# Decode attention of a hybrid MLA decoder step: keys as the moving operand, with heads on PSUM partitions

## The reference, cut to what matters

```python
past_ckv = cache_ckv_l[page_table].reshape(db, -1, KV_LORA)
past_kr = cache_kr_l[page_table].reshape(db, -1, ROPE_DIM)
q_abs = jnp.einsum('bthd,khd->bthk', q_nope, w_uk)
s_past = jnp.einsum('bthk,bsk->bhts', q_abs, past_ckv) + jnp.einsum('bthr,bsr->bhts', q_rope, past_kr)
s_new = jnp.einsum('bthk,bsk->bhts', q_abs, ckv) + jnp.einsum('bthr,bsr->bhts', q_rope, kr)
...
sc = jnp.concatenate([s_past, s_new], axis=-1).astype(jnp.float32) * SM_SCALE
p = jax.nn.softmax(sc, axis=-1).astype(ckv.dtype)
o_lat = (jnp.einsum('bhts,bsk->bthk', p[..., :n_past], past_ckv)
         + jnp.einsum('bhts,bsk->bthk', p[..., n_past:], ckv))
o = jnp.einsum('bthk,khv->bthv', o_lat, w_uv)
```

## Time and profile before

| | us |
|---|---|
| runs before | 1612.63, 1633.86, 1609.82; median 1612.63 |
| span of the profiled execution | 1616.8 |
| TensorE matmuls, busy | 1483.7 (92% of the span) |
| VectorE, ScalarE, GpSimd, busy | 780.6, 651.9, 493.5 |
| output stage | from 1210 to the end |

### The profile page before, as it was taken

How to read it: one execution, slowest core, us unless ns; L and a number is a source line. 1 busy time by engine, 2 the same in 40 slices (tenths; PEclk the granted TensorE clock), 3 DMA queues, 4 the chain that set the end, 5 groups by cost and what they waited for, 6 DMA issues and landing times. The chain is left out here.

```text
span 1616.8 us, 24423 instructions
## 1 busy us (share of the span) xinstructions
PE 1483.7 (92%) x8584; PEld 1236.4 (76%) x8584; DVE 780.6 (48%) x1594; ACT 651.9 (40%) x1296; POOL 493.5 (31%) x423
## 2 busy tenths in 40 slices
PE   7787799999999589999999999999848999999997
PEld 1487689999998467777777787877627888888886
DVE  0587532223321677766676767664252333333333
ACT  0255322222110556565666666666631222222221
POOL 0355523232221524343443434343331111111100
PEclk9899899999999799999999999999957999999999
DMA  9243221111101200000000000000065144434310
GB/s 367 94 126 110 84 87 53 53 53 52 58 27 47 52 1 11 11 8 12 8 12 8 14 4 14 7 7 11 15 244 181 60 157 156 155 122 146 124 60 28
DMA packets 71502, 114.70 MB, mean 71 GB/s; under 512 B 33236, under 2 KB 50548, under 8 KB 69205
## 3 DMA queue, kind: packets, MB, share of 16 engines
q1 hardware_dynamic: 58782, 70.73, 13.8%
q0 software_dynamic: 3456, 27.26, 4.6%
q10 hardware_dynamic: 9168, 15.50, 2.7%
HBM read 90.95 MB, written 22.77 MB: 70 GB/s over the span
## 5 line engine op out<-in xcount | busy, mean ns | idle before, releaser
L1177 POOL TENSOR_TENSOR pt_lo<-pt,pt_hi 128x512 fp32r<-128x512 f32 (+2 forms) x160 | 171.1, 1069 | 262.3 <-ACT pt_hi L1082 261.9
L1081 ACT ACTIVATE pt<-att_ps_s 128x512 f32<-128x512 f32 (+1 forms) x320 | 170.2, 532 | 150.9 <-PE att_ps_s L1351 85.3
L1237 DVE TENSOR_REDUCE mx<-att_ps_p 128x1 f32<-128x512 f32 (+2 forms) x300 | 177.2, 606 | 91.7 <-PE att_ps_p L1321 71.4
L1082 ACT ACTIVATE pt_hi<-att_ps_s 128x512 fp32r<-128x512 f32 (+1 forms) x320 | 169.2, 529 | 0.0
L1248 DVE TENSOR_TENSOR pt_lo<-pt,pt_hi 128x512 fp32r<-128x512 f32 (+1 forms) x160 | 120.2, 751 | 93.0 <-ACT pt_hi L1082 91.2
L107 PE MATMUL mix_ps_u<-mix_h_hi,wb_hi 128*128 128x256 f32 x512 | 146.2, 285 | 0.0
L109 PE MATMUL mix_ps_u<-mix_h_hi,wb_lo 128*128 128x256 f32 x512 | 144.9, 283 | 0.0
L108 PE MATMUL mix_ps_u<-mix_h_lo,wb_hi 128*128 128x256 f32 x512 | 144.9, 283 | 0.0
L107 PE MATMUL att_ps_o<-pt_hi,v_hi 128*128 128x512 f32 (+1 forms) x320 | 126.9, 397 | 9.3 <-DVE pt_lo L1248 8.5
L107 PE MATMUL out_ps_y<-wo_hi,mixed_hi 128*128 128x512 f32 x256 | 119.4, 466 | 2.6 <-POOL mixed_lo L1938 2.6
L1349 PE MATMUL att_ps_s<-q_hi,k_hi 97*128 97x512 f32 (+1 forms) x320 | 120.3, 376 | 1.6 <-issue 1.6
(11 more groups left out here) (348 smaller groups left out, 3316.2 us busy)
## 6 DMA issues: line engine op xcount, KB each, us to landing
ada<-in_ada_w_dram SPq DMA_DIRECT2D x8, 1536.0 KB, 15.1
lat_x<-in_x_prompt_dram SPq DMA_DIRECT2D x16, 512.0 KB, 4.3
mix_x<-in_x_prompt_dram SPq DMA_DIRECT2D x16, 512.0 KB, 3.7
x_rows<-in_x_prompt_dram SPq DMA_DIRECT2D x16, 512.0 KB
out_dram<-y ACTq DMA_DIRECT2D x16, 512.0 KB, 2.7
lat_wraw<-in_w_in_dram POOLq DMA_DIRECT2D x8, 768.0 KB
gate_att_scratch<-gate_a SPq DMA_DIRECT2D x16, 256.0 KB, 2.0
pool_scratch<-mixed SPq DMA_DIRECT2D x32, 128.0 KB, 2.0
```

The lines of the kernel that those rows point to most:

```text
L1081: act.activation(pt[:, k % 2, 0:n], ps_s[:, k % 2, 0:n], ACT.Exp, scale=SCALE)
L1082: act.activation(ph[0][:, k % 4, 0:n], ps_s[:, k % 2, 0:n], ACT.Exp, scale=SCALE).then_inc(exp_done, 1)
L1177: pool.tensor_tensor(ph[1][:, k % 4, 0:n], pt[:, k % 2, 0:n], ph[0][:, k % 4, 0:n].bitcast(F32), ALU.subtract).then_inc(p_lo_ready[1], 1)
L1237: dve.tensor_reduce(mx[:, I % 2, r, c:c + 1], chunk_bank(g, n)[:, 0:width], AX.X, ALU.max).then_inc(chunk_read, 1)
```

## The change

Queries become the stationary operand and keys the moving one, so that scores lie as heads x tokens. The 32 tokens of a partition are split among four groups of 32 output partitions: token 4a + g goes to partitions 32g to 32g + 7. `score` runs twice per sample: one matmul of the rotary keys for all groups (512 columns, a 128x128 stationary operand in blocks), then four of the latent keys (8 stationary columns, 512 moving), one to each group of output partitions. The softmax takes one maximum per partition, folds the four groups, and applies scale and shift in one exponential over 1024 columns, with its sum. The exponentials are transposed back (`turn_exp`, 8 transposes), copied by `keep_exp`, and `values` streams 128 columns of the cache past 8 stationary weights, 32 calls to the four groups in turn. `fold_values` adds the groups up. All of this now lies in the sample's own body, at fixed units; pieces are turned two at a time. The last sample has no order of its own; `project` and `turn_mixed` follow the last body. The zeroed operand `ms` is replaced by reused buffers, and half of the small matmuls at the end of the set-up go away. The gather is issued one block earlier.

```diff
@@ set-up @@
-            for part in ms:
-                last = pool.memset(part[:].bitcast(F32), 0.0)
...
-            kept(dve.tensor_copy(new_col[:], ps_r[0:H, 0:DB]))
...
-                pe.matmul(ps_r[0:H, n:n + 1], qabs[:, n, :], lat_c[:, QC, n:n + 1], start=True, stop=False)
-                last = pe.matmul(ps_r[0:H, n:n + 1], qr[0:ROPE, n, 0, :], krt[:, n:n + 1], start=False, stop=True)
@@ order of a body @@
-        stride = 1 if last else 2
-        names = ("tile_maxima", "turn_maxima", "head_maxima", "spread", "shift", "exp", "sum")
-        at = dict(zip(names, range(stride * NI + 2, UNITS)))
+    PIECES = [("r", half, 0) for half in range(HALVES)] + [("t", half, g) for half in range(HALVES) for g in range(GRP)]
+    TURN_AT = {1 + 2 * k: (2 * k, 2 * k + 1) for k in range(NI // 2)}
+    SCORE_AT = {8: 0, 12: 1}
+    names = ("tile_maxima", "turn_maxima", "head_maxima", "spread", "shift", "exp", "turn_exp", "keep_exp",
+             "values0", "values1", "keep_out", "fold")
+    AT = dict(zip(names, (13, 16, 16, 18, 18, 18, 24, 24, 26, 28, 29, 31)))
@@ ScalarE @@
+            def exponentials(s):
+                act.wait_ge(negb_ready, s + 1)
...
+                act.activation(pn[:, :, 0:H], pn[:, :, 0:H], ACT.Exp)
+                act.activation(pr[:].rearrange("p a n -> p (a n)"), ps_s[:].rearrange("p a n -> p (a n)"), ACT.Exp,
+                               scale=SCALE, bias=negb[:], accum_out=dsum[:]).then_inc(exp_ready, 1)
@@ GpSimd @@
-                if n % 2 == 1 and 1 <= s < DB - 1:
+                if n % 2 == 0 and 1 <= s < DB - 1:
@@ VectorE @@
+            def tile_maxima(s):
+                dve.wait_ge(scored, HALVES * s + HALVES)
+                dve.tensor_reduce(mx[:], ps_s[:].rearrange("p a n -> p (a n)"), AX.X, ALU.max).then_inc(mx_ready, 1)
...
+            def shift(s):
+                dve.wait_ge(negb_done, s + 1)
+                dve.tensor_copy(negb[:], ps_m[:, NEGB:NEGB + 1]).then_inc(negb_ready, 1)
+            def keep_exp(s):
+                dve.wait_ge(exp_turned, s + 1)
+                dve.tensor_copy(prt[:], ps_s[:].rearrange("p a (c g r) -> p (a c) g r", c=GRP, g=GRP)[:, :, :, 0:H]).then_inc(prt_ready, 1)
+            def keep_out(s):
+                dve.wait_ge(pv_done, s + 1)
+                dve.tensor_copy(vo[:], ps_m[:, VALS:VALS + KVL])
...
+            def keep_latent(s):
+                dve.wait_ge(olat_done, s + 1)
@@ TensorE @@
+            def score(s, e, half):
...
+                for k in range(2):
+                    pe.wait_ge(piece_kept[k], NI // 2 * s + pieces_before(half, k))
+                pe.matmul(ps_s[:, half, :], qr_s[:, e].rearrange("p g r -> p (g r)"), crt[:, half, :], start=True, stop=False, skip_group_check=True)
+                for g in range(GRP):
+                    last = pe.matmul(ps_s[g * ROPE:g * ROPE + H, half, :], qabs_s[:, e, :], ckt[:, g, :],
+                                     start=False, stop=True, skip_group_check=True)
+            def turn_exp(s):
+                pe.wait_ge(exp_ready, s + 1)
...
+            def values(s, e, half):
+                if half == 0:
+                    pe.wait_ge(prt_ready, s + 1)
+                for a in range(half * GRP, (half + 1) * GRP):
+                    for g in range(GRP):
+                        pe.matmul(ps_m[g * ROPE:g * ROPE + H, VALS:VALS + KVL], prt[:, a, g, :], ck[e][:, a * GRP + g, :],
+                                  start=(a == 0), stop=(a == QT - 1 and g > 0), skip_group_check=True)
+            def fold_values(s):
+                pe.wait_ge(out_ready, s + 1)
+                pe.matmul(ps_m[:, OLAT:OLAT + H], vo[:], fold_r[:], start=True, stop=True, skip_group_check=True).then_inc(olat_done, 1)
...
             peeled(pe, DB // 2, lambda i: [body(2 * i + e, e) for e in range(2)])
+            project(range(H))
+            turn_mixed()
```

## The result

The kernel before ran in 1612.47 us (median of 4 runs), the changed kernel in 1551.95 (median of 4 runs, 1546.94 to 1556.66). The ratio on record is 0.9587 with a 95% interval of 0.9523 to 0.965: 4.1% faster (the two medians alone would give 0.9625), where the forecast was 1591 and its range of 8 in 10 ended at 1562. The profiled execution has a span of 1548.9 against 1616.8.

The account below looks back on a forecast made before the run. TensorE's queue was taken to bound the output stage. A body falling from 46.0 to 43.1 us gave -23.2 over eight, once-only terms +1.8: 1612.6 - 21.4, forecast 1591 us (-1.3%), 8-in-10 range 1562 to 1644.

Parts of the forecast that it names:

- the overlap of column groups: Scores and values on TensorE: calls to four groups overlap partly, four latent calls taking 2.18 us, between 0.87 and 3.49.
- Side by side: Rival for scores and values: all four groups run at once, body 40.5 us, time 1570; chance 0.13.
- changes of shape: On TensorE, 0.1 us whenever the array shape in use changes, as before and behind the four latent calls.
- the floor of 0.062 for each matmul: In the values: no matmul below 0.062 us, so 64 of them cannot go below 4.0.
- one after another: Rival for scores and values: column groups never overlap, body 48.7 us, time 1636, slower; chance 0.28.
- the two waits: TensorE waits 0.65 us at `turn_exp` for ScalarE's exponentials and 1.2 at `values` for `keep_exp`, 1.85 a body.
- the long exponential: ScalarE's exponential over 1024 columns, priced as the squares at 1.24 us, in the chain before `turn_exp`.
- small terms of TensorE: In a body: among others pieces 3.6 us, eight transposes of the exponentials 0.7, `fold` 0.2, `spread` 0.4.
- Once only: Terms outside the eight bodies: set-up -0.9, start of the stage +1.7, end +1.0; together +1.8 us.
- 0.9 was expected to be saved: In the set-up: half of VectorE's 0.81 us wait for TensorE's small matmuls goes, with one copy: -0.9.
- +1.7: Start of the output stage: VectorE's first copy is demanded two units sooner behind the gates' load, +1.4 to 2.8 us.

Follow-up runs that it names:

- both_one_group: Changed kernel with latent scores and values all written to the first group of output partitions, so nothing overlaps: 1632.0 us.
- before_again: A further profile of the kernel before, at a lower mean granted clock (0.936); no time is given.
- before_gates_late: Kernel before with VectorE's wait for the samples' gates moved from the stage's start to the tail: 0.9979 of the kernel before, interval 0.9908 to 1.005.

## Why the prediction was wrong

**The step that failed** is the overlap of column groups: "if matmuls start in order, the second of one call can only run beside the first of the next call". Side by side, the rival with a chance of 0.13, is what happened. The four latent calls took 0.97 instead of 2.18, a half's scores 0.96 + 0.97 = 1.93 instead of 3.25 (that rival had 1.94, with 0.1 for each of two changes of shape): -2.6 a body. The values took 1.98 a sample instead of 4.3: -2.3. Here a second step failed, the floor of 0.062 for each matmul. It was a misreading: 0.062 is 0.99 / 16 of `project`, which holds the 0.12 that its block costs once; the columns' 0.0545 is about all that one of its matmuls costs besides. Without the floor the forecast would have had 3.6 + 0.3 = 3.9; the other 1.9 is the overlap. The floor also kept the rival's own time, 1570, too slow by 8 x 2.3 = 18. `new_value` took 0.93 instead of 1.15. Another reading was wrong without harm to the sum: not only loads of the whole array ran ahead in the kernel before, as `project`'s loads of 8 columns did too (16 within 0.88 us, beside its matmuls). The Trainium skill, "TensorE: Matmul & The Clock Gate", Part 3, has matmuls start strictly in program order, which would give my 2.18; the windows above, with four matmuls under way first, do not agree for calls to different groups. Its span model in the same part, several tiles ending little later than one, agrees (0.97 for four calls, where the one call of the rotary keys took 0.96 and four calls in one group 3.53).

**Right:** the price of one after another. The rival said a body of 48.7 and 1636; `both_one_group` measured 48.4 and 1632.0. Also right were the two waits, their places and their causes: 0.93 and 0.53 by removal, against 1.2 and 0.65. They were priced a little too high: the long exponential took 1.09 and not 1.24; the rest was not traced.

**Too low:** small terms of TensorE. `turn_exp` took 0.85 instead of 0.7 (1361.57 to 1362.42). A body without waits is 36.70; 41.25 less 2.6, 2.3 and 0.2 would be 36.1. So 0.6 of small terms was missed, 0.15 of it at `turn_exp`, 0.4 at the pieces, of which a pair took 0.8 and not 0.72 (1335.10 to 1335.90).

**Once only:** between the two profiles, what lies outside of eight bodies is 67.9 - 62.7 = 5.2 in favour, where 1.8 against was forecast. The largest part is luck. The first body of the kernel before took 48.53 without any values, so 46.0 - 7.55 = 38.45 of work and 10.1 of start, against 3.0 in the first profile after: 7.1, by the gates' load.

A second part, 3.2, is one body of the kernel before at a lower clock; 6.8 us of it are at 0.50, the lower of TensorE's two levels (1.2 GHz), with TensorE busy throughout:
```profile
1311.20:1360.41 49.21, 48.75 (x298) 42.70 (x297) 16.24 (x29) 11.09 (x20) 7.10 (x6) 0.93 0.37 129
1339.30:1346.10 6.80, 6.80 (x28) 6.09 (x26) 0.20 (x2) 1.83 (x4) 2.06 (x2) 0.50 0.94 336
```
That is hardly chance: `before_again` and `before_gates_late` each have one such body too (49.18, granted 0.93), the drop again 27 to 28 us into it, and none of the 15 profiles of the changed kernel and its variants has one. It seems to belong to the order before, so that the change gains it; why the clock falls there no run shows.

The rest is against the change. 0.9 lies ahead of the stage's first piece, where 0.9 was expected to be saved; but that piece starts anywhere from 1215.1 to 1220.7 in those 15 profiles, so neither is shown. 2.3 lies in the last body: it had two samples' values before and took 53.29, 0.3 less than its prices (46.0 + 7.55), and takes 40.17 now, 2.0 more than the others. 1.8 lies in the tail, 21.0 instead of 19.2 at a granted clock of 0.78. 3.2 + 7.1 - 0.9 - 2.3 - 1.8 = 5.3. By medians of runs the bodies' 62.7 face 60.5, so the once-only sum is 2.2 against, near the +1.8 of the forecast; but the start alone moves a run by more than that, and its +1.7 is neither confirmed nor refuted.

With the measured scores, values and new value in place of mine the forecast would have been 1591 - 8 x 5.2 = 1549. That it lies so near is partly luck: the small terms were 0.6 a body too low and the waits 0.4 too high.

## What to carry to other kernels

Small-output float32 matmuls (here 8 stationary columns) are worth spreading over the four groups of output partitions even when they stream many columns: four streams cost what one costs, if the program takes the groups in turn and gives none more than four matmuls in a row. Price an overlap by who shares what, not by program order, and where no row shows it, give both ends an honest chance. After a large gain on the bound engine, look for the waits that it exposes, and for a wait on data that is used much later.

## What was not expected of the hardware

- Matmuls to different groups of output partitions pass each other in TensorE's queue. A queue of four matmuls for each group fits five orders of the values (0.99, 1.02, 1.66, 2.30 and, with one group, 3.59 a half), one of them forecast; how it is built was not shown.
- Eight weight loads of 8 columns for four groups were done within 0.12 us, so four of them lay a whole matmul ahead of their use; in one group two came at the start and the others 0.43 apart.
- One small load, the samples' gates, took 8.0 to 14.9 us from issue to use in profiles of this stage. Six runs of the changed kernel spread over 9.5 us with the wait for it at the start, six over 3.2 with the wait in the tail.
- In all three profiles of the kernel before and its variant the granted clock fell to half for 6.8 us inside a body in which TensorE was busy; in none of 15 profiles of the changed order.
